# Stage borders of a hybrid decoder step on one core: when GpSimd counts a stage as closed, and who waits for its transfers

## The chip, the cores and the metric

The kernel runs on one core of a Trainium2 chip. The metric is device time in microseconds (us), the median of several runs. A core has TensorE (PE in the profile; PEld is its weight loading), VectorE (DVE), ScalarE (ACT), GpSimd (POOL) and SyncE (SP), each with an instruction stream of its own. They meet through semaphores only. Transfers between HBM and the on-chip SBUF are issued by SyncE, ScalarE or GpSimd and land later by themselves. In the profile's rows POOLq, SPq and so on are the sequencers of these engines.

## The reference

One step of a small decoder: a gated DeltaNet layer, a ConvFFN, a native-sparse-attention (NSA) layer and a second ConvFFN, for a prompt of 256 tokens and for 8 sequences of 8 new tokens with 1024 tokens of past each. Cut to what matters here:

```python
def trunk(x, ...):
    for i in range(DEPTH):                       # DEPTH = 2
        if i % 2 == 0:
            y, s_new, cb = gdn_mixer(x, gdn_state[j], ...)   # delta rule; writes new states
        else:
            y, rows, wb = nsa_mixer(x, past_kv, nsa_win[j], ...)  # writes new key/value rows and windows
        x = x + y
        y, fb = conv_ffn(x, ffn_conv[i], ...)
        x = x + y
    return rms_norm(x, final_norm), rows, win, states, ...

def gdn_mixer(...):
    o, s_new = chunk_gated_delta(q, k, v, g, beta, s0)       # the "core"
    o = rms_norm(o, out_norm_w) * jax.nn.silu(z)             # the "gate norm"
    return o.reshape(b, t, GDN_V_DIM) @ w_out, s_new, new_buf

def nsa_mixer(...):
    proj = rms_norm(x, norm_w) @ w_in                        # "project"
    cmp_k = compress_blocks(...); cmp_v = compress_blocks(...)
    # for each block of queries: attention over compressed rows, over the selected
    # blocks of 64 rows, and over the window of 512 rows; gated sum of the three
    return out @ w_out, new_rows, new_win
```

The new delta-rule states, the new key/value rows and the shifted windows are outputs too, so they are stored to HBM while the step goes on.

## The kernel before

All tokens, 256 of the prompt and 64 of the samples, are kept as 320 columns, with features on the 128 partitions. Large products run through a ring of four weight slots: SyncE loads a unit of weights (`stream`, L551), ScalarE rounds it (`high_part`, L582), VectorE takes the rest (`low_part`, L597), and TensorE makes three products of the parts (L621 to L623).

The program is a row of stages, in the same order on every engine. Each engine adds 1 to the semaphore `stage_closed` when it has done with a stage, in most places by `drain().then_inc(...)`, which holds the engine's stream until its own earlier instructions are through. At some borders every engine then waits for four times the number of the stage, as TensorE, ScalarE, VectorE and GpSimd are the four that count. The order of work inside a stage is the order in which each engine's function is written; a `Fori` is a hardware loop. Five stages matter here.

- The core (stage 4, `pe_core`, `act_core`, `dve_core`, `pool_core`): eight rounds of two heads of the delta rule, with the compression of the cached keys and values woven in. SyncE stores the new states (L1032, L1033; semaphore `state_out`) and the compressed keys and values (L1036, L1038; `cmp_out`), then goes on, without a border of its own, to the weights of gdn_out. GpSimd ends its part with waits for all these stores (L1527 to L1529) and then drains.
- The gate norm (from the fourth border on): ScalarE squares the heads (L1587), TensorE sums the squares (L1604), ScalarE takes the root (L1589) and rounds the first two units of weights (L582, written over memory that the core's states used), VectorE takes the reciprocal (L1622), TensorE spreads it (L1610), and VectorE multiplies.
- The rows (stage 8, `pool_rows` on GpSimd, L2086 on): the other engines compress the prompt's keys and values and turn the new rows to tokens (the last of them are `g8` of VectorE and `g7` of ScalarE). GpSimd loads the second half of the compression weights (L1912), the compressed keys and values (L2088, L2089; `cmp_in`), waits for the last rows, issues eleven stores of rows (L2095 to L2099), and then `load_keys(pool, 0)`: it reads the eight page numbers of the first sequence (L1941) and issues eight page loads (L1946; `k_in`) and a window load (L1950; `kw_in`).
- The attention (stage 9, "mixed"): TensorE turns the keys of a sequence (`pe_turn_keys`, L2226; it waits for `k_in` and `kw_in`), one sequence ahead of the one attended to. GpSimd loads the keys of the next sequence in a loop (`pool_mixed`, L2201) once the turned ones are out of the way. SyncE waits for the eighth border and then loads each sequence's values (L2192).
- The output product of the attention and the second ConvFFN follow.

Of the kernel before, what the change touches and what calls it, by code (L numbers as in the profile page):

```python
# [37 lines left out]
QKH, VH, DK = 8, 16, 128  # L38
# [190 lines left out]
def build(nc, ins, outs, where, base_cols):  # L229
    ctx = ExitStack()  # L230
    with ctx:
# [78 lines left out]
        stage_closed = sem("stage_closed")  # L310
# [493 lines left out]
        def dve_gdn_in(dve):  # L804
# [6 lines left out]
            for u in range(NCT // 2 + 2, 24):  # L811
# [15 lines left out]
                  act=steps("gates_act", ["nbexp", "sq0", "sq1", "sq2", "sq3", "abs", "expn", "root", "log", "ea", "egap", "eg"]))  # L827
# [690 lines left out]
        def pool_core(pool):  # L1518
            pool.sem_inc(S5["pool"].sem, S5["pool"].first)
            for v in range(2):  # L1520
                if v:
                    pool_core_pair(pool, 0, 4, 1, split=True)
                with pool.Fori(v, 4) as g:
                    pool_core_pair(pool, g, g + 4 * v, v)
            pool.wait_ge(state_out, STATES * QKH + 16)
            for v in range(2):
                pool.wait_ge(cmp_out[v], 8 * UNITS_CMP + 16)  # L1527
# [55 lines left out]
        def act_gate_norm(act):  # L1583
            for g in range(8):
                if g >= 2:
                    act.wait_ge(S6["pe"].sem, S6["pe"].count(f"sum{g - 2}"))
                act.activation(sq6[g % 2], o_heads[:, 2 * g:2 * g + 2, :], ACT.Square).then_inc(S6["act"].sem, S6["act"].step(f"sq{g}"))  # L1587
            act.wait_ge(S6["pe"].sem, S6["pe"].count("sum7"))
            act.activation(inv16, psum[0:VH, 0, 0:T], ACT.Sqrt, bias=eps_col[0:VH, :], scale=1.0 / DK).then_inc(S6["act"].sem, S6["act"].step("root"))  # L1589
            for u in range(2):  # L1590
                high_part(act, "gdn_out", 0, u, VH, free=True)
            for j in range(VH):
                act.wait_ge(S6["dve"].sem, S6["dve"].count(f"out{j}"))
                act.copy(o_hi[:, j, :], z[:, j, :]).then_inc(x_hi, 1)
            high_part(act, "gdn_out", 0, 2, VH)
            norm_f0.act_adding(act, VH)
            norm_f0.act_root(act)
# [222 lines left out]
        def nsa_stages():  # L1820
# [118 lines left out]
            def load_keys(pool, it, pages_free=None, window_free=None):  # L1939

                pages = [pool.value_load(pages_sb[0:1, bass.ds(NPG * it + g, 1)], min_val=0, max_val=NPOOL - 1) for g in range(NPG)]  # L1941
                if pages_free is not None:
                    pages_free()
                for g in range(NPG):
                    src = kv_rows[bass.ds(pages[g], 1)].rearrange("o s c -> (o s) c")
                    pool.dma_start(k_sel[:, g, :], src[:, K_SEL]).then_inc(k_in, 16)  # L1946
                w = win_rows[bass.ds(it, 1)].rearrange("o p t c -> (o p) t c")
                if window_free is not None:
                    window_free()
                pool.dma_start(k_win, w[:, :, 0:KV_DIM]).then_inc(kw_in, 16)  # L1950
# [135 lines left out]
            def pool_rows(pool):  # L2086
                load_w1_again(pool, 1)
                pool.dma_start(ckT, ck_dram).then_inc(cmp_in, 16)  # L2088
                pool.dma_start(cv, cv_dram).then_inc(cmp_in, 16)  # L2089

                pool.wait_ge(R["dve"].sem, R["dve"].count("g8"))
                pool.wait_ge(R["act"].sem, R["act"].count("g7"))
                kvp = outs["kv_rows_prompt"].rearrange("l b (t p) c g d -> p (l b t) (c g d)", p=P)
                wp = outs["win_prompt"].rearrange("l b (t p) c g d -> p (l b t) (c g d)", p=P)
                pool.dma_start(kvp, rows_p[:, :, 0:4 * KV_DIM]).then_inc(stored, 16)  # L2095
                pool.dma_start(wp, rows_p[:, :, 4 * KV_DIM:]).then_inc(stored, 16)
                pool.dma_start(outs["kv_rows_sample"].rearrange("l b q c g d -> (l b q) (c g d)"), rows_s[:, 0:4 * KV_DIM]).then_inc(stored, 16)
                for b in range(NB):
                    pool.dma_start(outs["win_sample"][0, b].rearrange("w c g d -> w (c g d)")[WIN - TQ:, :],  # L2099
                                   rows_s[b * TQ:(b + 1) * TQ, 4 * KV_DIM:]).then_inc(stored, 16)  # L2100
                n_stored[0] += 11
                load_keys(pool, 0)
                pool.wait_ge(cmp_in, 32)


            o_tok = space.take(2, 2, Q_DIM // 2, off=ring_at + 2 * SLOT)
# [297 lines left out]
            def act_mixed(act):  # L2404
                act.sem_inc(M["act"].sem, M["act"].first - 1)
                act.wait_ge(zeroed, 2)
                act_take_pair(act, 0).then_inc(M["act"].sem, 1)
                act_take_q(act, 0)
                act_turn_keys(act, 0, 0, first=True)
                act_turn_keys(act, 1, 0, first=True)  # L2410
                act_compressed(act, 0)
                for n in range(2, 6):
                    act_turn_keys(act, n, 0, first=True)
                act_take_values(act, 0)
                with act.Fori(0, 4) as i:
                    act_mixed_part(act, i)
                with act.Fori(4, LAST) as i:
                    act_mixed_part(act, i)
                act_mixed_part(act, LAST, last=True)

            def act_take_pair(act, it):
                return act.copy(qs, one(qT[:, bass.ds(it, 1), 0:TP]))
# [487 lines left out]
        @block.gpsimd  # L2910
        def _(pool):
            project, rows, mixed = nsa["pool"]
            pool.sem_inc(stage_closed, 1)
            pool_gdn_in(pool)
            pool.drain().then_inc(stage_closed, 1)
            pool.wait_ge(stage_closed, 4 * 2)
            pool.sem_inc(stage_closed, 1)
            pool.wait_ge(bias_pe, 1)
            for m in range(8):
                split_w1(pool, 0, m)  # L2920
            pool.wait_ge(stage_closed, 4 * 3)
            pool_core(pool)
            pool.drain().then_inc(stage_closed, 1)
            pool.wait_ge(stage_closed, 4 * 4)
            pool.sem_inc(stage_closed, 1)
            ffns[0]["pool"](pool)
            pool.sem_inc(stage_closed, 1)
            project(pool)
            pool.drain().then_inc(stage_closed, 1)
            pool.wait_ge(stage_closed, 4 * 7)  # L2930
            rows(pool)
            pool.drain().then_inc(stage_closed, 1)
            pool.wait_ge(stage_closed, 4 * 8)
            mixed(pool)
            pool.drain().then_inc(stage_closed, 1)
            pool.wait_ge(stage_closed, 4 * 9)
            pool.sem_inc(stage_closed, 1)
            ffns[1]["pool"](pool)
            fin["pool"](pool)
# [34 lines left out]
```

## Time and profile before

| | us |
|---|---|
| median of 3 runs | 1716.98 |
| lowest and highest run | 1714.06, 1723.23 |
| span of the profiled execution (a device time of its own is not given for it) | 1715.5 |
| TensorE busy in the span | 1539.0 (90%) |
| VectorE, ScalarE, GpSimd busy | 952.5, 800.6, 300.1 |

The span runs from the first to the last instruction of one execution. The busy shares are averages over stages with quite different limits. The chain that ended last is followed back from the last instruction to what released each step, so it shows which engine or transfer held the end at each moment; the timeline and the windows show the same stretch from the side of each engine.

### The profile page before, as it was taken

To read this page: it belongs to the slowest core of one execution; us is meant where nothing else is said; L and a number is where in the kernel's file an instruction comes from. 1 tells how busy PE (TensorE), PEld (TensorE's weight loads), DVE (VectorE), ACT (ScalarE), POOL (GpSimd) and SP (SyncE) were. 2 spreads that over 40 slices of the span, in tenths; PEclk is the share of its full clock that TensorE was granted. 3 is DMA by queue.
4 is the path that set the end of the run, shared out by engine and by line. 5 is a ranking of instruction groups with operands and counts; after the bars stand their busy time and mean duration, and the time that the engine had idled before them with its cause. 6 is when DMAs were issued, how large, how long until landed. Compare 5 with 4: busy or idle time off the path is not lost.

```text
span 1715.5 us, 38118 instructions
## 1 busy us (share of the span) xinstructions
PE 1539.0 (90%) x13678; PEld 1348.7 (79%) x13678; DVE 952.5 (56%) x1749; ACT 800.6 (47%) x1579; POOL 300.1 (17%) x492
## 2 busy tenths in 40 slices
PE   6999979999988998899999999966777778999897
PEld 6999847777757776579999999954555558999897
DVE  5775245554655454464777644434655556777732
ACT  5675325665555555443444533224444535444521
POOL 1331033433454332200000001031112100000000
PEclk9999969999999998979999999997898987999999
DMA  7444232322432232425555658444534414555650
GB/s 179 147 144 157 102 117 58 95 76 59 125 100 71 66 89 75 112 66 147 148 147 147 174 134 227 128 151 143 169 98 161 132 50 123 147 147 147 164 135 31
DMA packets 285294, 209.56 MB, mean 122 GB/s; under 512 B 29231, under 2 KB 277071, under 8 KB 284768
## 3 DMA queue, kind: packets, MB, share of 16 engines
q1 hardware_dynamic: 275926, 176.32, 36.9%
q0 software_dynamic: 9248, 31.80, 6.0%
q8 instruction: 45, 0.74, 0.2%
q10 hardware_dynamic: 42, 0.44, 0.1%
q14 instruction: 33, 0.27, 0.1%
HBM read 185.67 MB, written 22.85 MB: 122 GB/s over the span
## 4 chain that ended last, share of the span: by engine, by line
PE 74%; DVE 8%; ACT 7%; issue 5%; DMA 2%; SPq 1%; POOL 1%; POOLq 1%; DVEq 0%; ACTq 0%
PE psum L621 15%; PE psum L622 15%; PE psum L623 15%; PE psum L1107 7%; ACT sbuf_resident L2429 2%; PE psum L1221 1%; PE psum L2226 1%; PE psum L1091 1%; PE psum L2381 1%; DMA sbuf_resident<-in_nsa_w_in_dram 1%; PE psum L1610 1%; PE psum L915 1%; PE psum L1270 1%; PE psum L1234 1%; PE psum L1250 1%
## 5 line engine op out<-in xcount | busy, mean ns | idle before, releaser
L621 PE MATMUL psum<-h_rounded,weights_low 128*128 128x320 f32 x1248 | 392.0, 314 | 1.9 <-DVE weights_low L597 1.9
L623 PE MATMUL psum<-h_rounded,weights_high 128*128 128x320 f32 x1248 | 387.0, 310 | 0.0
L622 PE MATMUL psum<-weighted_x_low,weights_high 128*128 128x320 f32 x864 | 267.2, 309 | 0.0
L621 PEld LDWEIGHTS psum<-h_rounded,weights_low 128*128 128x128 f32 x1248 | 235.2, 188 | 5.1 <-DVE weights_low L597 2.1
L597 DVE TENSOR_TENSOR weights_low<-sbuf_resident,weights_high 128x2048 fp32r<-128x2048 f32 x90 | 205.7, 2288 | 55.1 <-ACT weights_high L582 55.1
L623 PEld LDWEIGHTS psum<-h_rounded,weights_high 128*128 128x128 f32 x1248 | 235.1, 188 | 0.0
L582 ACT CAST weights_high<-sbuf_resident 128x2048 fp32r<-128x2048 f32 x90 | 170.1, 1893 | 95.1 <-PE psum L623 64.8
L622 PEld LDWEIGHTS psum<-weighted_x_low,weights_high 128*128 128x128 f32 x864 | 165.9, 192 | 0.2
L1143 ACT COPY sbuf_resident<-psum 64x256 f32<-64x256 f32 x256 | 108.5, 424 | 91.3 <-PE psum L1091 88.8
L696 DVE SCALAR_TENSOR_TENSOR sbuf_stages<-sbuf_stages,sbuf_resident 128x344 f32<-128x344 f32 (+1 forms) x184 | 105.6, 574 | 55.5 <-ACT sbuf_stages L678 51.7
L1543 POOL TENSOR_TENSOR turned_low<-sbuf_resident,turned_high 128x512 fp32r<-128x512 f32 x64 | 76.8, 1200 | 265.3 <-ACT turned_high L1146 265.2
L678 ACT ACTIVATE sbuf_stages<-sbuf_stages,sbuf_resident 128x336 f32<-128x336 f32 (+1 forms) x76 | 44.1, 581 | 165.0 <-DVE sbuf_stages L1774 164.0
L622 PE MATMUL psum<-weights_low,weights_high 128*128 128x320 f32 x384 | 118.8, 309 | 0.0
L686 POOL COPY sbuf_stages<-sbuf_stages 128x2 f32<-128x2 f32 (+1 forms) x76 | 30.8, 405 | 494.5 <-DVE sbuf_stages L1774 417.8
L621 PE MATMUL psum<-hidden_high,weights_low 128*128 128x320 f32 x352 | 110.9, 315 | 6.3 <-ACT sbuf_resident L1731 5.4
L1107 PE MATMUL psum<-turned_high,w_low 128*128 128x504 f32 x256 | 114.6, 448 | 1.9 <-POOL w_low L1535 1.9
L622 PE MATMUL psum<-hidden_low,weights_high_wide 128*128 128x320 f32 x352 | 110.0, 313 | 0.0
L623 PE MATMUL psum<-hidden_high,weights_high_wide 128*128 128x320 f32 x352 | 109.8, 312 | 0.0
L1107 PE MATMUL psum<-turned_high,w_high 128*128 128x504 f32 x256 | 106.6, 416 | 0.0
L1107 PE MATMUL psum<-turned_low,w_high 128*128 128x504 f32 x256 | 75.1, 400 | 2.8 <-POOL turned_low L1543 2.8
L1645 DVE TENSOR_TENSOR sbuf_resident<-sbuf_resident,psum 128x320 f32<-128x320 f32 x24 | 11.7, 487 | 118.1 <-PE psum L623 118.1
L622 PEld LDWEIGHTS psum<-weights_low,weights_high 128*128 128x128 f32 x384 | 73.4, 191 | 0.0
(438 smaller groups left out, 3147.7 us busy)
## 6 DMA issues: line engine op xcount, KB each, us to landing
sbuf_resident<-in_ffn_w_up_dram SPq DMA_DIRECT2D x88, 512.0 KB, 4.9
sbuf_resident<-in_gdn_w_in_dram SPq DMA_DIRECT2D x48, 512.0 KB, 4.7
sbuf_resident<-in_ffn_w_down_dram SPq DMA_DIRECT2D x32, 704.0 KB, 6.3
sbuf_resident<-in_cache_nsa_kv_dram SPq DMA_DIRECT2D x256, 64.0 KB
sbuf_stages<-in_state_gdn_s_dram POOLq DMA_DIRECT2D x16, 512.0 KB, 5.3
out_gdn_s_sample_dram<-sbuf_stages SPq DMA_DIRECT2D x16, 512.0 KB, 3.8
sbuf_resident<-in_gdn_w_out_dram SPq DMA_DIRECT2D x16, 512.0 KB, 5.5
sbuf_stages<-in_cache_nsa_kv_dram POOLq DMA_DIRECT2D x64, 128.0 KB, 3.4
```

The source lines that it names most:

```text
L582: act.copy(dst[:, 0:kn * P], slot(w)[:, 0:kn * P]).then_inc(hi_done, 1)
L597: eng.tensor_tensor(ring_lo[w % RING][:, 0:kn * P], sl, hi[:, 0:kn * P], ALU.subtract).then_inc(lo_done, 1)
L621: pe.matmul(out, w_lo, x_hi_tile, start=first, stop=False)
L622: pe.matmul(out, w_hi, x_lo_tile, start=False, stop=False)
L623: return pe.matmul(out, w_hi, x_hi_tile, start=False, stop=last)
L678: return act.activation(y[:, 0:n_out], xp[:, 0:n_out], ACT.Copy, scale=tap)
L686: pool.tensor_copy(tail[:, 0:hist], xp[:, TP:TP + hist])
L696: dve.scalar_tensor_tensor(out=y[:, 0:n_out], in0=xp[:, n:n + n_out], scalar=taps(n), in1=y[:, 0:n_out], op0=ALU.mult, op1=ALU.add).then_i ...
L1107: last = pe.matmul(psum[:, H_BANK[t], 0:4 * NC2], weights[:, 8 * half + m, t * P:(t + 1) * P], rows, start=(m == 0 and half == 0 and part ...
L1143: last = act.copy(dst, src)
L1543: pool.tensor_tensor(turned_low[m % TURNED], turned[m % TURNED], turned_high[m % TURNED], ALU.subtract).then_inc(pool_steps.sem, pool_step ...
L2429: return act.activation(s, s, ACT.Exp, bias=mx_p[:, h, x:x + 1], accum_out=sm_p[:, h, x:x + 1])
```

## The change

GpSimd reports earlier, and those who need what it has in flight wait for that themselves.

- At the core's end GpSimd drains and counts first, and waits for the stores of states and compressed rows after that. ScalarE waits for the states' stores before its first rounding of gdn_out weights.
- In the row stage GpSimd counts the stage as soon as it has passed the border before, without a drain, and does not stop at the next border; it goes from `rows` straight to `mixed`. At the end of `mixed` it counts without a drain.
- The key loads of the first sequence are issued ahead of the wait for the last rows and of the stores. The wait for the compressed keys and values moves from GpSimd to ScalarE, in front of its first use of them.

```diff
--- before.py
+++ after.py
@@ -1522,6 +1522,8 @@
                     pool_core_pair(pool, 0, 4, 1, split=True)
                 with pool.Fori(v, 4) as g:
                     pool_core_pair(pool, g, g + 4 * v, v)
+
+        def pool_core_stored(pool):
             pool.wait_ge(state_out, STATES * QKH + 16)
             for v in range(2):
                 pool.wait_ge(cmp_out[v], 8 * UNITS_CMP + 16)
@@ -1587,6 +1589,7 @@
                 act.activation(sq6[g % 2], o_heads[:, 2 * g:2 * g + 2, :], ACT.Square).then_inc(S6["act"].sem, S6["act"].step(f"sq{g}"))
             act.wait_ge(S6["pe"].sem, S6["pe"].count("sum7"))
             act.activation(inv16, psum[0:VH, 0, 0:T], ACT.Sqrt, bias=eps_col[0:VH, :], scale=1.0 / DK).then_inc(S6["act"].sem, S6["act"].step("root"))
+            act.wait_ge(state_out, STATES * QKH + 16)
             for u in range(2):
                 high_part(act, "gdn_out", 0, u, VH, free=True)
             for j in range(VH):
@@ -2087,6 +2090,7 @@
                 load_w1_again(pool, 1)
                 pool.dma_start(ckT, ck_dram).then_inc(cmp_in, 16)
                 pool.dma_start(cv, cv_dram).then_inc(cmp_in, 16)
+                load_keys(pool, 0)
 
                 pool.wait_ge(R["dve"].sem, R["dve"].count("g8"))
                 pool.wait_ge(R["act"].sem, R["act"].count("g7"))
@@ -2099,8 +2103,6 @@
                     pool.dma_start(outs["win_sample"][0, b].rearrange("w c g d -> w (c g d)")[WIN - TQ:, :],
                                    rows_s[b * TQ:(b + 1) * TQ, 4 * KV_DIM:]).then_inc(stored, 16)
                 n_stored[0] += 11
-                load_keys(pool, 0)
-                pool.wait_ge(cmp_in, 32)
 
 
             o_tok = space.take(2, 2, Q_DIM // 2, off=ring_at + 2 * SLOT)
@@ -2405,6 +2407,7 @@
                 act.sem_inc(M["act"].sem, M["act"].first - 1)
                 act.wait_ge(zeroed, 2)
                 act_take_pair(act, 0).then_inc(M["act"].sem, 1)
+                act.wait_ge(cmp_in, 32)
                 act_take_q(act, 0)
                 act_turn_keys(act, 0, 0, first=True)
                 act_turn_keys(act, 1, 0, first=True)
@@ -2921,6 +2924,7 @@
             pool.wait_ge(stage_closed, 4 * 3)
             pool_core(pool)
             pool.drain().then_inc(stage_closed, 1)
+            pool_core_stored(pool)
             pool.wait_ge(stage_closed, 4 * 4)
             pool.sem_inc(stage_closed, 1)
             ffns[0]["pool"](pool)
@@ -2928,11 +2932,10 @@
             project(pool)
             pool.drain().then_inc(stage_closed, 1)
             pool.wait_ge(stage_closed, 4 * 7)
+            pool.sem_inc(stage_closed, 1)
             rows(pool)
-            pool.drain().then_inc(stage_closed, 1)
-            pool.wait_ge(stage_closed, 4 * 8)
             mixed(pool)
-            pool.drain().then_inc(stage_closed, 1)
+            pool.sem_inc(stage_closed, 1)
             pool.wait_ge(stage_closed, 4 * 9)
             pool.sem_inc(stage_closed, 1)
             ffns[1]["pool"](pool)
```

In the first place, GpSimd's stream in the row stage before (the names are those of the tensors; `page_rows` are the page numbers, and a semaphore that an instruction waits for stands in brackets):

```order
L1912 DMA sbuf_stages<-in_nsa_cmp_w_dram 128x16x256 [waits attention_tables_in,stage_closed]
L2088 DMA sbuf_stages<-compressed_keys 128x1008
L2089 DMA sbuf_stages<-compressed_values 63x2048
L2095 DMA out_kv_rows_prompt_dram<-sbuf_stages 128x2x1024 [waits rows_act,rows_dve]
L2096 DMA out_win_prompt_dram<-sbuf_stages 128x2x512
L2097 DMA out_kv_rows_sample_dram<-sbuf_stages 64x1024
L2099 DMA out_win_sample_dram<-sbuf_stages 8x512 x8
L1941 TENSOR_LOAD page_rows
L1941 ISA x2
...
L1946 DMA sbuf_stages<-in_cache_nsa_kv_dram 128x256
...
L1950 DMA sbuf_stages<-in_cache_nsa_win_dram 128x4x256
L2201 UNCONDITIONAL_BRANCH [waits compressed_in,stage_closed]
```

and now:

```order
L1915 DMA sbuf_stages<-in_nsa_cmp_w_dram 128x16x256 [waits attention_tables_in,stage_closed]
L2091 DMA sbuf_stages<-compressed_keys 128x1008
L2092 DMA sbuf_stages<-compressed_values 63x2048
L1944 TENSOR_LOAD page_rows
L1944 ISA x2
...
L1949 DMA sbuf_stages<-in_cache_nsa_kv_dram 128x256
...
L1953 DMA sbuf_stages<-in_cache_nsa_win_dram 128x4x256
L2099 DMA out_kv_rows_prompt_dram<-sbuf_stages 128x2x1024 [waits rows_act,rows_dve]
L2100 DMA out_win_prompt_dram<-sbuf_stages 128x2x512
L2101 DMA out_kv_rows_sample_dram<-sbuf_stages 64x1024
L2103 DMA out_win_sample_dram<-sbuf_stages 8x512 x8
L2203 UNCONDITIONAL_BRANCH
```

The page numbers, the key loads and the window load have moved ahead of the stores and of the wait for the last rows (`rows_act`, `rows_dve`), and the loop of the attention (the branch at the end) has lost its wait for the border and for the compressed tensors.

In the second place, ScalarE's stream in the gate norm before (squares, root, the first two rounded weight units, the gated values):

```order
L1587 ACTIVATE sbuf_stages<-sbuf_stages 128x640
L1587 ACTIVATE sbuf_stages<-sbuf_stages 128x640 [waits gate_norm_pe] x6
L1589 ACT_TABLE_LOAD
L1589 ACTIVATE sbuf_stages<-psum,sbuf_stages 16x320 [waits gate_norm_pe]
L582 CAST weights_high_53<-sbuf_resident 128x2048 [waits weights_in_slot0]
L582 CAST weights_high_54<-sbuf_resident 128x2048 [waits weights_in_slot1]
L1594 CAST gated_high<-sbuf_stages 128x320 [waits gate_norm_dve] x16
```

and now:

```order
L1589 ACTIVATE sbuf_stages<-sbuf_stages 128x640
L1589 ACTIVATE sbuf_stages<-sbuf_stages 128x640 [waits gate_norm_pe] x6
L1591 ACT_TABLE_LOAD
L1591 ACTIVATE sbuf_stages<-psum,sbuf_stages 16x320 [waits gate_norm_pe]
L582 CAST weights_high_53<-sbuf_resident 128x2048 [waits weights_in_slot0,states_out]
L582 CAST weights_high_54<-sbuf_resident 128x2048 [waits weights_in_slot1]
L1597 CAST gated_high<-sbuf_stages 128x320 [waits gate_norm_dve] x16
```

Nothing has moved there; the first rounding of weights also waits for `states_out`.

## Rows read from the trace of the kernel before

**Rows 1.** The page: the span, and the chain that ended last by engine.

```profile
span 1715.5 us, 38118 instructions
...
PE 74%; DVE 8%; ACT 7%; issue 5%; DMA 2%; SPq 1%; POOL 1%; POOLq 1%; DVEq 0%; ACTq 0%
```

**Rows 2.** Chain around the core's border: start, length (both us), engine and line.

```profile
714.13 3.88 DMA compressed_values<-sbuf_resident
...
718.30 0.75 ACT sbuf_stages L1587
...
719.18 10.57 PE psum L1604 x32
```

**Rows 3.** Timeline there: start, length, engine, line, operation, [idle before <-releaser].

```profile
712.23 0.74 ACT L1161 COPY sbuf_resident<-psum 63x256 f32<-63x256 f32 x2 [1.32 <-PE psum L1132]
...
730.20 3.68 ACT L582 CAST weights_high<-sbuf_resident 128x2048 fp32r<-128x2048 f32 x2
...
732.52 16.94 PE L1610 MATMUL psum<-sbuf_stages,sbuf_resident 16*128 16x320 f32 x32 [2.78 <-DVE sbuf_stages L1622]
```

**Rows 4.** Two-us windows: busy us of PE, PEld, DVE, ACT, POOL; clock; DMA share; GB/s.

```profile
714.00:716.00 2.00, 0.00 (x0) 0.00 (x0) 0.00 (x0) 0.00 (x0) 0.00 (x0) 1.00 1.04 293
716.00:718.00 2.00, 0.00 (x0) 0.00 (x0) 0.00 (x0) 0.00 (x0) 0.00 (x0) 0.50 0.77 205
...
722.00:724.00 2.00, 2.00 (x8) 0.54 (x5) 2.00 (x2) 0.93 (x2) 0.00 (x0) 0.80 1.19 288
...
734.00:736.00 2.00, 2.00 (x5) 1.20 (x5) 2.00 (x1) 0.46 (x1) 0.00 (x0) 0.50 0.00 0
```

**Rows 5.** The first eight issues of the gdn_out weights (L551) and their landing.

```profile
L551 SPq DMA_DIRECT2D sbuf_resident<-in_gdn_w_out_dram x8: 395/1542/1728, 715.7 to 725.9; - x8
...
DMA to landing us min/median/max: 4.7/7.1/7.3
```

**Rows 6.** Timeline of GpSimd in the row stage and behind it.

```profile
1126.95 0.56 POOL L2089 DMA_DIRECT2D sbuf_stages<-compressed_values  x1
1139.07 0.73 POOL L2095 DMA_DIRECT2D out_kv_rows_prompt_dram<-sbuf_stages  x1 [11.56 <-DVE sbuf_stages L2065]
...
1141.08 3.98 POOL L2099 DMA_DIRECT2D out_win_sample_dram<-sbuf_stages  x8
1150.59 4.72 POOL L1946 DMA_DIRECT2D sbuf_stages<-in_cache_nsa_kv_dram  x8 [5.53 <-issue]
1155.30 0.76 POOL L1950 DMA_DIRECT2D sbuf_stages<-in_cache_nsa_win_dram  x1
```

**Rows 7.** Timeline of VectorE: copies early in the row stage, its end, the attention's start.

```profile
1125.68 2.80 DVE L2023 COPY sbuf_stages<-sbuf_stages 64x128 f32<-64x128 f32 x8
...
1148.67 0.41 DVE L2084 COPY sbuf_stages<-psum 15x256 f32<-15x256 f32 x1 [0.88 <-PE psum L2010]
...
1160.54 0.30 DVE L2513 MEMSET sbuf_stages<- 128x128 f32 x2 [11.46 <-POOLq L2932]
```

**Rows 8.** Chain from the row stage's end on: start, length, engine and line.

```profile
1155.31 5.04 POOLq L2932
...
1160.90 1.98 PE psum L2226 x8
...
1167.25 1.06 PE psum L2226 x4
...
1173.13 6.23 DMA sbuf_stages<-in_cache_nsa_kv_dram
```

**Rows 9.** Landing times: the first window-key load (L1950), then the compressed values (L2089).

```profile
DMA to landing us min/median/max: 4.1/4.1/4.1
...
DMA to landing us min/median/max: 12.4/12.4/12.4
```

**Rows 10.** Windows as in rows 4: start of the attention stage, a stretch of the last FFN.

```profile
1160.50:1179.00 18.50, 14.15 (x93) 8.95 (x93) 8.20 (x25) 9.89 (x33) 5.06 (x9) 0.56 0.62 194
...
1620.00:1628.00 8.00, 6.39 (x26) 6.39 (x27) 6.09 (x2) 6.44 (x4) 1.03 (x2) 0.57 0.57 117
```

## The prediction

> **What bounds the kernel now.** I read the chain that ended last before the busy shares. It shows a kernel with TensorE (PE) on 74% of its path [rows 1]. A gain must therefore come from places where the chain leaves every compute engine. I looked for such places at the stage borders, with the chain and the timeline, and found two that the change touches.
>
> Border A is the end of the delta-rule core. TensorE, VectorE, ScalarE and GpSimd (POOL) are all done at 712.97 us, with ScalarE last (712.23 + 0.74) [rows 3]. The next stage starts at 718.30. Between them the chain holds the transfer of the compressed values, issued at 714.13 and landed 3.88 us later, which GpSimd awaits before it reports [rows 2].
>
> Border B is the end of the row stage. VectorE is last off GpSimd, at 1149.08 (1148.67 + 0.41), and the attention starts at 1160.54 [rows 7]. GpSimd alone fills the time between: its stores' issues end at 1145.06, it reads page numbers for 5.53 us, issues eight key loads (4.72) and a window load (0.76), and sits in its drain for 5.04 us [rows 6, 8].
>
> **The change part by part.**
>
> *A, reporting ahead of the stores.* The border now opens with ScalarE's last copy. From the last work to the first of the next stage a border takes about 0.2 us (border B: the drain ends at 1160.35, the memset starts at 1160.54 [rows 7, 8]). So the stage opens at 712.97 + 0.2 = 713.2 instead of 718.30: **5.1 us**. GpSimd still waits for the landings at 718.0, but behind it in its queue are only its copies for the next FFN, which started at the old border too; nobody needs them during the gate norm.
>
> *A, the wait added on ScalarE.* It stands behind the square root and ahead of the first cast of gdn_out weights; queued behind it are that cast, the second cast and sixteen casts of gated values, for which VectorE and then TensorE wait. The states were issued before the compressed values, so they are in by about 718.0 [rows 2]. ScalarE arrives there at 730.20 - 5.1 - 1.8 = 723.3 (the 1.8 is the next step) [rows 3]. The wait costs nothing, with 5 us to spare.
>
> *A, weights.* The first cast needs unit 0 (issues 1 and 2), the second unit 1 (issues 3 and 4). The eight issues spread from 715.7 to 725.9, so about 1.46 us apart; the fourth leaves at about 720.1 and lands within 7.3 us, at 727.4 at worst; the first two lie in by about 722 to 724 [rows 5]. SyncE does not wait at this border, so these times stay. The casts took 3.68 us together [rows 3] and are wanted from 723.3: the second at 725.1. It may start up to 2.3 us late. Behind it stands only the first gated value; VectorE has a weights_low of its own to do first, which covers about 2 us. Cost between 0 and 2.3 us; I take 0.3.
>
> *A, TensorE's clock.* TensorE's last product of the core released ScalarE at 712.23 [rows 3]. The granted clock was still 1.00 in 714 to 716 and 0.50 (1.2 GHz) in 716 to 718, before it had work, and 0.80 on average in 722 to 724 [rows 4], so it was low from 716 to about 722.8 (a mean of 0.80 over 2 us is 0.8 us at 0.50). The square sums started at 719.18 [rows 2], so they had 722.8 - 719.2 = 3.6 us at the lower level, and half of that, 1.8 us, is what full clock gives back. Now the pause is 712.2 to about 714.1, and at 714 to 716 the clock had not yet fallen. Against it: after an idle of only 2.78 us, ahead of L1610, the clock was 0.50 from 734 on [rows 3, 4]. The pause of 1.9 lies below that. If the clock stays, I gain 1.8; if it falls with work in hand, nothing; if it stayed low for all 32 instructions they would take 10.57 + (10.57 - 3.6) = 17.5, a loss of 7.0. I take 1.8, since the observed fall came later after the stop than work will resume.
> The Trainium skill, "TensorE: Matmul & The Clock Gate" (What's actually happening), says that activity releases the throttle and that the array's default is 1.2 GHz. By that rule a shorter pause cannot hurt by itself, but it may not suffice; with the clock lost the sum below would be 1.8 us smaller.
>
> *B, GpSimd reports at the stage's start.* GpSimd's share of the count is given before it issues anything. The border opens with VectorE's last copy, at 1149.08 + 0.2 = 1149.3 instead of 1160.54: **11.2 us**.
>
> *B, the key loads moved up.* Moved are eight page-number reads, eight loads and a window load. They stood behind the eleven stores and now stand ahead of them, behind the loads of w1 and of the two compressed tensors. They took 5.53 + 4.72 + 0.76 = 11.0 us [rows 6]. They start at 1127.5 (1126.95 + 0.56) and end at 1138.5, just inside GpSimd's wait for the last rows, which ended at 1139.07. Thus the stores leave as before. The keys share the queue with w1 and the compressed tensors, which took until 1126.95 + 12.4 = 1139.4 to land [rows 9]. The window load took 4.1 us to land on an emptier queue [rows 9]; behind the queue that is 1139.4 + 4.1 = 1143.5 at worst, against a need at 1149.3. Cover: 5.8 us.
> The Trainium skill, "SBUF — State Buffer" (SBUF: two separate sides, and its note on VectorE blocking DMA), says that a fp32 SBUF-to-SBUF copy on VectorE keeps GpSimd from writing descriptors. It speaks against moving these issues beside VectorE's copies. Here the issue of L2089 took 0.56 us in the middle of eight such copies [rows 7], against 4.72 / 8 = 0.59 for a key load with VectorE idle [rows 6], so no loss is seen. By the rule the loads would slip, and the cover would shrink; it raises the chance of my first rival.
>
> *B, page numbers of sequence 1.* They are read after the stores: 1145.06 + 5.5 = 1150.6. The wait behind them is for TensorE's turning of the keys, which ended at 1168.31 (1167.25 + 1.06) [rows 8] and will end near 1157. It stays free. SyncE's value loads start with the border, so they move along with it.
>
> *B, the wait for the compressed tensors on ScalarE* stands behind the q copy; landed at 1139.4, wanted at 1149.5: nothing.
>
> *B, TensorE's clock.* The attention began cold: mean 0.56 over 1160.5 to 1179 [rows 10]. With a pause of 1 us it begins at 1.00. On the chain are eight instructions in 1.98 and four in 1.06 us [rows 8], at half clock; full clock saves 1.5 of these, some short ones perhaps 0.4 more. Then comes a load with 6.23 us to landing that no clock shortens [rows 8]. TensorE has little to do here and may lose the clock again. Between 0 and 1.9 (a loss is excluded: it is at the low level now); I take 1.0.
>
> *The last border (end of attention)*, where a drain goes: TensorE and ScalarE end that stage and GpSimd issues nothing there, 0.
>
> *Sum.* 5.1 - 0.3 + 1.8 + 11.2 + 1.0 = **18.8 us**. The span of 1715.5 [rows 1] becomes 1696.7. The profile gives no device time of its own execution; the median of the three runs, 1716.98, lies 1.5 above its span, and I keep that: **1698.2 us**. After both borders the program is a chain of waits among engines, and nothing in it keeps a fixed hour, so the gain should last to the end.
>
> **The rivals.**
>
> *Late keys and crowded transfers.* Key loads and stores are in flight together, and SyncE's value loads start while the last stores run. If the queue serves them slowly, the attention starts when the keys land. For: a window load and pages behind 12.4 us of queue [rows 9]; in the attention a key load already needed 6.23 us [rows 8]. Against: 5.8 us of cover. Price: were the 6.23 doubled and put behind the cover, about 6 us: 1704.
>
> *Weights late at A.* Full 2.3 us and the clock lost: 2.0 + 1.8 more than in my sum: 1702.
>
> *The border does not open.* Some other reporter holds it: the profile names GpSimd, but a wait for several is put down to the last, and SyncE's stores could hold VectorE or ScalarE by other semaphores. Then only one of the gains comes: with A alone 1698.2 + 12.2 = 1710.4, with neither 1717.
>
> *Slower: the clock in the long products.* TensorE runs the FFN weights nearly without pause, and every stretch at half clock there is on the path. One stretch exists: 0.57 over 8 us, 3.4 us lost [rows 10]. With less rest at both borders the chip could grant less. The change gives 18.8, and slower by over 0.5% (8.6) begins at 27.4, so from nine more such stretches (30.6 us): 1729. Nothing in the rows links a border to a stretch 450 us later.
>
> **How the numbers follow.** Forecast 0.66, crowded transfers 0.14, weights and clock 0.08, border shut 0.08, slower 0.04. What a measurement can tell from no change is about 0.5%, or 8.6 us: faster means below 1708.4. The first three cases (0.88) are faster; 0.08 is the same; 0.04 slower. Low end: both clock terms full (0.9 more), no late weights (0.3) and the spread of the three runs, 2.9 below their median: about 1694. High end: crowded transfers, 1704, and what a third of the loss bound of the clock at A (7.0) would add, 2.3, rounded up with the runs' spread: 1708.
>
> **What would show it.** In the profile after: squares start about 0.3 us behind ScalarE's last copy of the core; the square sums take near 8.8 us, with clock 1.00, or 10.5 if it fell; the first cast does not wait for states_out. GpSimd's eight key loads lie between 1133 and 1138 on the old scale and its stores begin with the last rows. VectorE's first memset of the attention comes 0.2 us behind its last copy, and TensorE's first turning waits for no key. I am wrong if TensorE waits on a key load there, if the sequence loop of the attention lengthens, or if the stores start more than a microsecond after the last rows and somebody waits for them.

## The result and the profile after

| | before | after |
|---|---|---|
| forecast | | 1698.2 (1694 to 1708) |
| comparison on one chip, 15 runs each: median | 1719.77 | 1715.91 |
| lowest and highest | 1712.06, 1732.29 | 1704.75, 1721.63 |
| ratio of the times, 95% interval | | 0.9949 [0.9927, 0.9972] |
| span of the profiled execution, its mean granted clock | 1715.5, 0.943 | 1715.1, 0.929 |

The change gains about half a per cent by this ratio (the means, 1721.9 and 1713.8, lie 8.0 us apart), where the forecast had 1.1%. The median lies outside the range. In the two profiled executions nothing is gained at all: 1715.5 and 1715.1. So the question is where 18.8 us went.

**At the core's border they came.** The timeline of the changed kernel (start, length, engine, line, operation, idle before), TensorE and then ScalarE:

```profile
712.52 8.77 PE L1607 MATMUL psum<-sbuf_stages 128*16 128x320 f32 x32 [1.87 <-ACT sbuf_stages L1589]
724.08 2.61 PE L1613 MATMUL psum<-sbuf_stages,sbuf_resident 16*128 16x320 f32 x6 [2.78 <-DVE sbuf_stages L1625]
...
710.78 0.74 ACT L1161 COPY sbuf_resident<-psum 63x256 f32<-63x256 f32 x2 [1.32 <-PE psum L1132]
711.64 1.36 ACT L1589 ACTIVATE sbuf_stages<-sbuf_stages 128x640 f32<-128x640 f32 x2
```

ScalarE squares 0.12 us behind its last copy (711.64 - 711.52) where it used to wait 5.3 us, and the square sums take 8.77 us instead of 10.57 [rows 2, 3]: full clock gave back the 1.8 forecast. Seen from the core's last copy, the spreading products start 7.0 us earlier (724.08 - 710.78 = 13.30, before 732.52 - 712.23 = 20.29); the core itself ended 1.45 earlier in this execution. Two-us windows of the changed kernel, as in [rows 4]:

```profile
716.00:718.00 2.00, 2.00 (x9) 0.76 (x8) 1.55 (x2) 1.43 (x2) 0.87 (x1) 1.00 1.10 317
...
724.00:726.00 2.00, 1.92 (x6) 1.27 (x7) 1.11 (x3) 1.85 (x2) 0.00 (x0) 0.77 1.22 290
732.00:736.00 4.00, 4.00 (x9) 2.12 (x8) 4.00 (x7) 1.08 (x3) 0.00 (x0) 0.50 0.00 0
```

The clock is 1.00 through the border, where before it had fallen at 716. It falls to 0.50 (1.2 GHz) within 724 to 726, after the spreading products have begun; before, too, it fell there a second time [rows 4].

**At the row stage's border they came too.** Timeline of VectorE, then of GpSimd, changed kernel:

```profile
1140.25 0.41 DVE L2087 COPY sbuf_stages<-psum 15x256 f32<-15x256 f32 x1 [0.88 <-PE psum L2013]
1140.97 0.31 DVE L2516 MEMSET sbuf_stages<- 128x128 f32 x2 [0.30 <-DVEq L2902]
...
1122.95 4.70 POOL L1949 DMA_DIRECT2D sbuf_stages<-in_cache_nsa_kv_dram  x8 [4.31 <-issue]
...
1130.67 0.72 POOL L2099 DMA_DIRECT2D out_kv_rows_prompt_dram<-sbuf_stages  x1 [2.27 <-DVE sbuf_stages L2068]
```

The border takes 0.31 us (1140.66 to 1140.97) instead of 11.46 [rows 7]. The keys are issued inside GpSimd's wait, 2.27 us of which is left, and the stores leave with the last rows. TensorE's first turning starts at 1141.33, before at 1160.90 [rows 8], 19.6 us earlier, and the chain shows no key load ahead of it.

**Then they go.** Four marks of the same work. ScalarE's copy in the first and the last pass of the attention's sequences, before and after:

```profile
1197.04 1.02 ACT L2465 COPY sbuf_resident<-psum 128x1024 f32<-128x1024 f32 x1
1411.48 1.01 ACT L2465 COPY sbuf_resident<-psum 128x1024 f32<-128x1024 f32 x1 [2.06 <-PE psum L2373]
```

```profile
1179.34 1.02 ACT L2468 COPY sbuf_resident<-psum 128x1024 f32<-128x1024 f32 x1
1406.51 1.01 ACT L2468 COPY sbuf_resident<-psum 128x1024 f32<-128x1024 f32 x1 [2.06 <-PE psum L2375]
```

The issue of the last output store, before and after:

```profile
1710.32 0.54 POOL L2741 DMA_DIRECT2D out_y_sample_dram<-sbuf_stages  x1
```

```profile
1702.97 0.54 POOL L2744 DMA_DIRECT2D out_y_sample_dram<-sbuf_stages  x1
```

The lead is 19.6 us at the first turning, 17.7 in the first pass, 5.0 in the last, 7.35 at the last store, and 0.4 at the end of the span. There are two large losses. The first lies between the attention's passes; windows of before and after (columns as in [rows 4]):

```profile
1180.00:1395.00 215.00, 156.30 (x1989) 112.37 (x1988) 126.57 (x324) 104.69 (x314) 30.33 (x54) 0.92 0.41 132
```

```profile
1180.00:1395.00 215.00, 166.70 (x1819) 119.79 (x1820) 119.14 (x304) 99.60 (x299) 29.80 (x54) 0.81 0.39 124
```

In the same 215 us TensorE is busier and does fewer instructions: its clock was 0.81 instead of 0.92. The transfers' share is no larger.

The second loss lies behind the last store. Before, the span ends 5.18 us after that store's issue begins; after, 12.13 us. The store lands in 4.3 us in both. Then comes one more drain of GpSimd, the one that ends its program. No edit touched it, and it is no line of any stage: it stands at L231, the line that opens the block around the whole program. Before and after (duration in ns min/median/max, start):

```profile
L231 POOLq DRAIN  x1: 451/451/451, 1714.8 to 1714.8; - x1
```

```profile
L231 POOLq DRAIN  x1: 7406/7406/7406, 1707.5 to 1707.5; - x1
```

The difference, 6.955 us, is the whole of the added 6.95.

### The profile page after: what moved, and what is told of

Read it like the earlier page. It is cut to its first block and busy times, and to the rows that moved or that the text cites. A ratio compares the mean times of both kernels' runs of the same rounds, so it can differ in the third digit from the quotient of the medians.

```text
span 1715.1 us, 38119 instructions
## 1 busy us (share of the span) xinstructions
PE 1550.5 (90%) x13678; PEld 1355.7 (79%) x13678; DVE 953.3 (56%) x1749; ACT 800.8 (47%) x1579; POOL 299.9 (17%) x492
```

## The experiments

Twelve kernels in three groups of four, each group on one chip beside the kernel before. Means stand beside the medians where the runs of a kernel are spread out. Each execution's mean granted clock was kept.

**The change again.** No edit.

> The whole change, run once more beside the others. Clock theory (the gains at both borders come in full and are lost again later to stretches of TensorE's lower level, which fall differently from run to run): a median again 4 to 9 us below before, runs spread over 10 us or more, and time falling as the mean granted clock rises, about 7 us per 0.01; a run at the clock of before's profiled execution (0.943) near 1707 or below. Transfer theory (keys, values and stores in flight together lengthen the attention's passes): the same median, but time independent of the clock. Chance theory (the first comparison happened to draw slow runs): a median near 1700.

Median 1713.03 (1707.05 to 1722.75), ratio 0.9937 [0.9909, 0.9965], mean 1714.2 against 1724.2. The gain is real and stays at 8 to 10 us. Over the 66 runs of before in the three groups time and clock go together (correlation -0.91, -7.6 us for +0.01); their mean is 1723.8, and the lowest was 1712.0. The clock theory's slope held (it said about 7 us), the chance theory fell. But the mean clock of before was 0.931 and of the changed kernel 0.934 and 0.932: the change does not lower the clock on average, so the clock cannot be what takes 10 us of it on average.

**Each border alone.** First the core's part:

```diff
+        def pool_core_stored(pool):
             pool.wait_ge(state_out, STATES * QKH + 16)
...
+            act.wait_ge(state_out, STATES * QKH + 16)
             for u in range(2):
...
             pool.drain().then_inc(stage_closed, 1)
+            pool_core_stored(pool)
```

> Only the core border's part (early report, the wait on ScalarE). In the trace: the gate norm's square sums start near 712.5 and the gated products (L1610 of before, at 732.5 there) near 724, 8 us early; the attention's first memset is early by the same 8 us and no more. Clock theory: the median lies 3 to 8 us below before, the rest taken or given by the clock. Transfer theory: the full 8 us arrive in every run, since no key or value transfer is touched: 1709 to 1712.

Median 1719.22 (1704.12 to 1733.2), ratio 0.9938 [0.9907, 0.997], mean 1716.4: 7.8 below before, with a standard error of 3.3. The one run at 1733.2 weighs in this: without it the mean is 1714.3, 9.9 below. The transfer theory's 1709 to 1712 in every run did not come. Then the rest of the change's diff, without these lines:

> Only the row stage's border (report at the stage's start, keys issued ahead of the stores, the wait for the compressed tensors on ScalarE, no drain at the end of the attention). In the trace: the attention starts 11 us early against its own row stage. Clock theory: 11 us at the attention's first pass in the trace, part of it gone in the passes where the granted clock is at its lower level, and a median between 0 and 11 us below before. Transfer theory: the passes are longer by the same amounts as in the whole change, also at full clock, and the median is within 3 us of before.

Median 1720.75 (1710.3 to 1727.26), ratio 0.9976 [0.9946, 1.0006], mean 1719.7: 4.5 below, of the 11.2 that its border opens earlier. In its trace VectorE's first memset came 0.31 us behind its last copy, and the passes followed each other by 30.2 to 30.7 us like those of before, so nothing was lost in them in this execution, and the longer passes of the transfer theory did not come. The last store was issued at 1697.47, yet the span ended at 1709.6, 12.1 us later. With the core's part alone it was 1697.17 and 1702.3, 5.1 later. The loss behind the last store belongs to the row border's part of the change.

That part takes two drains of GpSimd away and puts none in their place. What is left is the drain at L231: it took 7.406 us in this trace and 0.451 in that of the core's part alone.

**The clock held up.** 13 products a pass (7 in the last one), in three places where TensorE waits:

```diff
+                    pe.wait_ge(ds.sem, ds.count("oT1", i - 1))
+                    pe.wait_ge(A["dve"].sem, A["dve"].count("is", i))
+                    warm(pe, Z_BANK, 6)      # n times: matmul(psum[:, bank, 256:512], ident, kvT[:, 4, 0:TP])
                     pe.wait_ge(ds.sem, ds.count("ssn", i))
...
+                warm(pe, X_BANK[0], 2)
                 pe.wait_ge(as_.sem, as_.count("eb", i))
...
+                warm(pe, X_BANK[0], 5)
                 pe.wait_ge(as_.sem, as_.count("p1", i))
```

> The whole change, and in each attention pass 13 more products on TensorE (the identity against a tile of keys, 128 columns each, result read by nobody), put where TensorE waits for VectorE or ScalarE. They take about 0.2 to 0.25 us each at full clock, up to 3 us a pass, mostly inside waits. Clock theory: the granted clock of the attention stays near 1.00, the passes take 30 us or a little less, and the time falls to 1695 to 1704 with a smaller spread. Transfer theory: the clock rises and the passes stay at 31 to 33 us, the time stays at 1712 to 1720 or grows by what the added products cost.

Median 1707.47 (1697.55 to 1709.56), ratio 0.9879 [0.9847, 0.991], clock 0.951 on average. In the traces the clock of the window 1180 to 1395 was 0.93, where that of the change run again on the same chip was 0.81; it did not stay near 1.00. The clock theory was right that the passes at low clock cost time: the mean is 1706.1, 8.1 below that of the change run again. But 1695 to 1704 was too low; it left out the 7 us behind the last store. Each added product was of 256 columns, not of 128 as I had written beforehand.

**The drain put back, in the shade.** That is, where nobody waits for GpSimd:

```diff
             mixed(pool)
             pool.sem_inc(stage_closed, 1)
+            pool.drain()
...
             fin["pool"](pool)
+            pool.drain()
```

> The whole change, with a drain of GpSimd put back at the end of the attention, behind its report, where GpSimd has nothing to do for about 10 us before the last border (and one behind the very last store, so that this one has a line of its own). Backlog theory (a GpSimd drain takes time by the DMAs it has issued since its last one: 5.2 us for 64, so about 0.081 us each; the change left 91 of them to a drain behind the program's last stores, 7.4 us where before had 0.45): the drain at the attention's end takes 7.0 us hidden, the last one about 0.4, and the time falls by 7.0 us against the changed kernel: a median of 1704 to 1709, 14 to 18 below before. Clock theory alone (all that is missing went to the clock): no change from the changed kernel's 1711 to 1716.

Median 1707.53 (1696.47 to 1712.66), ratio 0.9891 [0.985, 0.9933], mean 1705.7. The two drains of this kernel, by line (duration in ns min/median/max, start):

```profile
L2939 POOLq DRAIN  x1: 7000/7000/7000, 1382.3 to 1382.3; - x1
```

```profile
L2944 POOLq DRAIN  x1: 451/451/451, 1708.3 to 1708.3; - x1
```

The drain takes 7.0 us at 1382.3, while the attention runs until 1413, and the last one is back at 0.45. The span ends 5.1 us behind the issue of the last store (1704.01, 1709.1). The mean is 19.3 below that of before on the same chip, and 8.3 below that of the changed kernel's 24 runs, which were not made beside it; 7.0 was expected.

**The last report alone.** The kernel before with one line changed:

```diff
             mixed(pool)
-            pool.drain().then_inc(stage_closed, 1)
+            pool.sem_inc(stage_closed, 1)
```

(and a drain behind the last store, to give it a line).

> The kernel before, with nothing changed but GpSimd's report at the end of the attention: given without the drain. Forecast of the prediction: 0, since GpSimd is not awaited there. Backlog theory: the last drain now stands for 64 + 5 = 69 DMAs and takes 69 * 0.081 = 5.6 us instead of 0.45, behind the last stores: 5.2 us slower than before, in every run, whatever the clock.

```profile
L2940 POOLq DRAIN  x1: 5612/5612/5612, 1714.8 to 1714.8; - x1
```

The drain is as foretold to 0.01 us. The time alone would not have shown it: median 1726.07, ratio 1.0009 [0.9983, 1.0035], an interval that holds both 0 and 5.2 us. These runs had a clock of 0.934 against 0.930; along each kernel's own line at 0.935 they stand at 1725.3 against 1721.2, 4.1 slower.

**The keys left behind the stores.** The row border's part once more, with one of its edits taken back:

```diff
                 pool.dma_start(cv, cv_dram).then_inc(cmp_in, 16)
-                load_keys(pool, 0)
...
                 n_stored[0] += 11
+                load_keys(pool, 0)
```

> The kernel before with GpSimd's report of the row stage given at its start, but the key loads left behind the stores (and the wait for the compressed tensors on ScalarE, and no drain at the attention's end). The border opens 11.2 us early all the same, but TensorE's first turning waits for the keys, whose loads are issued until about 1155.3 on before's scale and need some 4 us more to land: it starts near 1159.3 instead of 1160.9, 1.6 us gained, and the late drain costs 7.0: 5 us slower than before by the backlog theory; 1 to 2 faster without it. If the keys' place did not matter the attention would start at 1149.5.

Median 1729.03, ratio 1.0029 [1.0001, 1.0057], mean 3.9 above before: a little slower than before, where 5 was expected. TensorE's first turning in its timeline:

```profile
1158.63 1.94 PE L2225 MATMUL psum<-sbuf_resident,sbuf_stages 128*128 128x128 f32 x8 [8.81 <-DMA sbuf_stages<-in_cache_nsa_kv_dram]
```

The border opens (VectorE at 1150.57), and TensorE waits 8.8 us for a key load. It starts 8.4 us behind VectorE's last copy, before 11.8; 3.4 us gained instead of my 1.6, since the last key needed 2.5 us to land and not 4. With the keys moved the border gave 11.15 us, without it 3.4, less than the 7.0 of the late drain.

**Everything together.** b1, the products of a4, and twelve of the identity by itself ahead of the output projection:

```diff
             pe.wait_ge(stage_closed, 4 * 9)
+            for _ in range(12):
+                pe.matmul(psum[:, 7, 0:P], ident, ident, start=True, stop=True)
             project_out(pe)
```

> As b1, with 13 idle products of TensorE in each attention pass (identity by keys, result unread) and 12 (identity by identity) ahead of the output projection, where TensorE waits 4.9 us for weights. Backlog theory and clock theory together: 7.0 us below the kernel with the added products alone (mean 1706): 1697 to 1701, and about 1 to 4 us less where the projection's first units no longer run at half clock (they did for about 17 us in before, from 1426 on). If the added products near the projection gain nothing, its first products still take 0.27 us each.

Median **1695.76** (1694.33 to 1697.29), ratio 0.984 [0.9797, 0.9882]: the fastest kernel of this study. The projection's products started 0.15 us apart instead of 0.27, and the window over its start shows full clock, where the one of before, 1423 to 1443, had 0.76:

```profile
1405.00:1425.00 20.00, 18.07 (x130) 17.91 (x129) 16.19 (x21) 12.71 (x20) 0.00 (x0) 1.00 0.52 160
```

**The borders weighed with less noise.** The same added products in before (c1), in the changed kernel without the drain put back (c2), in the core's part (c3) and in the row border's part with the drain put back (c4), on one chip.

> The kernel before with the added idle products (13 in each attention pass, 12 ahead of the output projection), which in b3 held the granted clock up and the spread of the runs at 3 us. With that noise gone the two borders can be weighed alone. If they are worth what the forecast said without its clock terms (5.1 - 0.3 + 11.2 = 16.0), this kernel lies 16 above b3's 1695.8: 1711 to 1713; with the clock terms too (2.8), 1714.6. If the change were worth only the 8 to 10 us of the plain comparison even without the late drain, it would lie at 1704 to 1706. The last drain takes 0.45 us.

> The whole change with the same added products, and no drain put back: b3 without its drain. Backlog theory: the last drain, over 91 DMAs, takes 7.41 us against 0.45 in b3, and the run 7.0 more than b3's 1695.8: 1702 to 1704, spread as small. Clock theory alone: 1695 to 1697, as b3.

> Only the core border's part, with the added products; all drains as before. 5.1 for the early report, less 0 to 0.3, and 1.8 if the square sums at full clock are worth that to the end: 5 to 6.6 below c1_before_quiet, whatever that is.

> Only the row stage's border, with the drain put back at the attention's end, and the added products: 11.2 below c1_before_quiet, and up to 1 more for the attention beginning at full clock. The gains of c3 and c4 add up to what c1 lies above b3 (16 to 19).

| kernel | runs | median | mean | lowest to highest | below c1 (by means) |
|---|---|---|---|---|---|
| c1 before | 12 | 1717.84 | 1717.6 | 4.5 | |
| c3 core border | 9 | 1708.21 | 1707.6 | 16.0 | 10.0 |
| c4 row border, drain put back | 6 | 1703.31 | 1703.9 | 12.2 | 13.7 |
| c2 both, late drain | 6 | 1701.88 | 1702.0 | 5.6 | 15.6 |
| b3 both, drain put back (another chip) | 4 | 1695.76 | 1695.8 | 3.0 | 21.8 |

c2 lies 6.2 above b3, the late drain. Both borders without it are worth 15.6 + 7.0 = 22.6; the two alone add up to 23.7. c1 itself came out at 1717.8, not 1711 to 1713: I had set it 16 above b3, and by these means the borders were worth more. So was each alone: 10.0 where I expected 5 to 6.6, and 13.7 where I expected 11.2 to 12.2; their sum of 23.7 is above my 16 to 19. These two kernels kept their spread in spite of the added products, and each mean has a standard error of 1.8, so how the total splits between the borders is known only to some 2 us. The marks of c1 and c2, ScalarE's copy in the first and the last pass:

```profile
1201.28 1.02 ACT L2473 COPY sbuf_resident<-psum 128x1024 f32<-128x1024 f32 x1
1418.18 1.01 ACT L2473 COPY sbuf_resident<-psum 128x1024 f32<-128x1024 f32 x1 [1.18 <-PE psum L2380]
```

```profile
1180.75 1.02 ACT L2476 COPY sbuf_resident<-psum 128x1024 f32<-128x1024 f32 x1
1393.89 1.01 ACT L2476 COPY sbuf_resident<-psum 128x1024 f32<-128x1024 f32 x1 [1.18 <-PE psum L2382]
```

With the clock at 0.96 and 0.98 in the passes the lead is 20.5 us in the first pass and 24.3 in the last: nothing is lost. The 3.8 more are not a gain of the borders but go with the clock: three passes of c1 took 31.9 to 32.0 us and one of c2, the others 29.8 to 30.4. The lead in the first pass is what the pair of plain profiles had hidden.

## Why the prediction was wrong

**Right: both borders and their places.** The core's border gave 5.2 us (5.1 foretold) and the square sums 1.8 (1.8). The second cast waited 0.51 us for its weights (0.3 taken), and nothing behind it moved; the wait for the states on ScalarE cost nothing. The row stage's border gave 11.15 us (11.2), the keys' nine issues stayed inside GpSimd's wait, and nobody waited for keys, compressed tensors or the page numbers of sequence 1. From the start of the core's last copy (713.41 in c1, 712.50 in c2) to the first pass's copy the quiet pair needs 487.87 and 468.25 us: 19.6 less, against my sum of 18.8.

**Mis-sized: the clock of the attention's start, 1.0.** TensorE came to the changed kernel's border at 1.00, but in the first 18.5 us of the attention its mean clock was 0.69, where before had 0.57. From the first turning to the first pass's copy it took 36.14 us before and 38.01 after, 1.9 more instead of 1.0 less; in the quiet pair 38.88 and 38.36, 0.5 less.

**The step that failed: "The last border (end of attention), where a drain goes: TensorE and ScalarE end that stage and GpSimd issues nothing there, 0."** It was right that nobody waits for GpSimd there, and wrong that the drain was free to drop. Its 5.2 us went with the 64 DMAs that GpSimd had issued since the drain before, and they passed in the shade of the attention; the row stage's 22 DMAs had a drain of their own, inside the wait at that border. With both drains gone the cost stands at the next one, and that is the one behind the program's last stores: 7.41 us for 91 DMAs instead of 0.45 for 5, so 6.95 us on the path. The sentence that closed the sum, "nothing in it keeps a fixed hour, so the gain should last to the end", fell with it. Put right, the sum is 18.8 - 7.0 = 11.8; measured, by means, were 8.0 and 10.0, and with the drain put back 19.3 (1725.0 and 1705.7).

**The base was a lucky one.** I set the 18.8 us against 1716.98, the median of three runs, and a profiled execution with a clock of 0.943. The mean of 66 runs of before is 1723.8 with a clock of 0.931. So 6.8 us of the miss lie in the base: 1698.2 + 6.8 + 7.0 = 1712.0, and the changed kernel's 24 runs have a mean of 1714.0 (15 of 1713.8, 9 of 1714.2). The 2.0 left over are about one and a half standard errors of these means. My "spread of the three runs, 2.9" was far too small for a kernel whose runs lie 20 us apart.

**The rivals.** Crowded transfers did not come: the share of the transfers fell, and passes at full clock were as short as before. The border opened. The slower case, less clock in exchange for less rest, looked right in the single pair of profiles (0.81 against 0.92 in the passes, 12.7 us lost), and is not borne out by the runs' clocks. I gave "faster" 0.88; before and after differ by 0.5%, just at the bound, and the range missed because neither a late drain nor the base was in it.

**Open.** Whether beginning the attention warm changes how often its passes fall to the lower level was not settled; the difference would be small beside the spread. What exactly a GpSimd drain counts is open too (below), and so is the split of the gain between the borders to better than 2 us.

## What to carry to other kernels

A drain, or any wait on a queue that is taken off one place, leaves its work to the next place that has it: look for the next drain on that engine, down to the one that ends the program, and leave one where the engine has nothing to do. Compare marks of the same work (first pass, last pass, last store, end of the span) before believing that a gain came or went; the total alone showed here neither the gain of 19.6 nor the loss of 7.0, and the lead of a single pair of profiles was blurred by the clock. The row that names the loss, the last drain, stood in the first pair of profiles, under a line far from any that had been changed. And where runs spread by more than the effect, first quiet them, or put each time beside its clock, and take the base from many runs.

## What the runs showed of the hardware

- GpSimd's drain grows with the DMAs that it has issued since its last one: 0.046 us for none (b1, the drain behind its own last one), 0.451 for 5, 5.202 for 64, 5.612 for 69, 7.000 for 86, 7.403 or 7.406 for 91, the same to a few ns in each kernel. That is about 81 ns for each, output stores and key loads alike, even long after the transfers have landed: before, the last key load was issued at 1356.3, and the drain began at 1393.6.
- It is not the whole rule. The drain at the core's end follows 16 loads of GpSimd and took 0.14 us before, not the 1.3 that 16 would give. After the change it took 4.56 us there, but only because it now began while GpSimd still worked: it ended at 706.15, 0.16 us behind GpSimd's last operation. The drain before the row stage, after 6 DMAs, took 6.9 to 7.8 us; in the kernel before it ended 0.3 us behind the landing of the compression weights (1048.57 + 15.4 = 1063.97; 1057.06 + 7.19 = 1064.25). After the row stage's 22, with transfers in flight, it took 5.1 to 5.7.
- The Trainium skill, "VectorE: DVE Perf Modes" (The DRAIN you can't avoid), says that the drains which the runtime adds around a program are a constant 12 ns or so on all engines. The drain at L231 took 7 ns on SyncE and 451 or 7406 ns on GpSimd, by what had been issued. Whether it is one of those that the page means is not shown; if it is, the constant does not hold for GpSimd.
- TensorE's granted clock stayed at 1.2 GHz while it had work without a pause: in the spreading products, of 16 rows, it was 0.50 from 726 to 745 in the changed kernel (19.00 us busy of 19.00), and from 734 to 752 before (18.00 of 18.00). A like stretch stands in every trace of this study. Being busy was not enough. With products of full height added in the pauses of the attention the clock in its passes was 0.93 instead of 0.81; whether the height is what matters was not tested.
- 98 products read by nobody made the changed kernel faster by 8.1 us (means 1714.2 and 1706.1 on one chip). With the projection's twelve the runs of three kernels lay 3 to 6 us apart, but those of two others 12 and 16, where those of the changed kernel lay 16 to 17 apart.
